# A two-block layer with product-key experts on one core: the last block of weights kept on the chip, three gelu places, and a thinner start of the choice

## What is computed

```python
q = (hb @ w_q).reshape(n, 8, 2, 128)
s = jnp.einsum('nhid,hikd->nhik', q, sub_keys)
s_top, i_top = lax.top_k(s, 16)
cand = s_top[:, :, 0, :, None] + s_top[:, :, 1, None, :]
cand_idx = i_top[:, :, 0, :, None] * 128 + i_top[:, :, 1, None, :]
best, pos = lax.top_k(cand.reshape(n, 8, 256), 16)
idx = jnp.take_along_axis(cand_idx.reshape(n, 8, -1), pos, axis=-1)
w = jax.nn.softmax(best, axis=-1)
u = jnp.take(u_tab, idx, axis=0)
act = jax.nn.gelu(jnp.einsum('nhkd,nd->nhk', u, hb))
out = jnp.einsum('nhk,nhkd->nd', w * act, jnp.take(v_tab, idx, axis=0))
```

## Time and profile before

| | us |
|---|---|
| Median of three runs (3157.71, 3168.16, 3169.7) | 3168.16 |
| The profiled execution: its own time | 3162.28 |
| The profiled execution: its span in the trace | 3160.5 |
| TensorE matmul busy | 3016.7 |
| VectorE busy | 2151.8 |
| ScalarE busy | 1230.4 |
| GpSimd busy | 439.8 |

### The profile page before, as it was taken

The page is one execution under the profiler, slowest core; times in us unless marked ns, Lnnn a source line. Parts: engine busy times, 40 slices in busy tenths (PEclk is TensorE's granted clock), DMA queues, the critical chain, the costliest instruction groups (busy, mean ns, idle before and its releaser), DMA issues. The chain is left out here.

```text
span 3160.5 us, 43420 instructions
## 1 busy us (share of the span) xinstructions
PE 3016.7 (95%) x17739; PEld 2766.1 (88%) x17739; DVE 2151.8 (68%) x3633; ACT 1230.4 (39%) x1936; POOL 439.8 (14%) x296
## 2 busy tenths in 40 slices
PE   7998998999999999999999999899999979999998
PEld 7888887888879888998877879799999979999998
DVE  6446875755643443577663468897987768889897
ACT  2234233222233341555553223366665733333332
POOL 0000000000000000000000000021113335555551
PEclk9888998999999998999999999999999989999999
DMA  6223113223232223212124333558888999999996
GB/s 234 102 101 147 41 44 117 76 91 107 78 130 81 74 107 128 81 68 79 69 100 166 121 120 124 196 203 274 278 268 311 344 359 379 392 392 393 393 392 234
DMA packets 221957, 584.19 MB, mean 185 GB/s; under 512 B 32704, under 2 KB 131520, under 8 KB 186304
## 3 DMA queue, kind: packets, MB, share of 16 engines
q1 hardware_dynamic: 178128, 422.42, 37.3%
q0 software_dynamic: 41472, 151.01, 13.0%
q10 hardware_dynamic: 2160, 7.99, 0.7%
HBM read 510.63 MB, written 70.25 MB: 184 GB/s over the span
## 5 line engine op out<-in xcount | busy, mean ns | idle before, releaser
L591 PE MATMUL bank<-hh,wh 128*128 128x512 f32 (+2 forms) x2512 | 907.8, 361 | 19.7 <-DVE wl L546 9.4
L591 PE MATMUL bank<-hl,wh 128*128 128x512 f32 (+2 forms) x2512 | 878.4, 350 | 0.0
L591 PE MATMUL bank<-hh,wl 128*128 128x512 f32 (+2 forms) x2512 | 877.4, 349 | 0.0
L539 ACT ACTIVATE wh<-ring 128x2048 fp32r<-128x2048 f32 (+2 forms) x249 | 463.6, 1862 | 765.1 <-PE bank L591 756.5
L546 DVE TENSOR_TENSOR wl<-ring,wh 128x2048 fp32r<-128x2048 f32 (+2 forms) x249 | 554.3, 2226 | 299.8 <-ACT wh L539 299.2
L591 PEld LDWEIGHTS bank<-hh,wh 128*128 128x128 f32 x2512 | 481.0, 191 | 70.7 <-issue 18.4
L591 PEld LDWEIGHTS bank<-hl,wh 128*128 128x128 f32 x2512 | 481.2, 192 | 45.7 <-issue 6.0
L591 PEld LDWEIGHTS bank<-hh,wl 128*128 128x128 f32 x2512 | 479.7, 191 | 42.8
L591 PE MATMUL bank<-ph,wh 128*128 128x368 f32 x1024 | 342.8, 335 | 30.8 <-DVE pl L3284 30.8
L591 PE MATMUL bank<-pl,wh 128*128 128x368 f32 x1024 | 340.6, 333 | 0.0
L591 PE MATMUL bank<-ph,wl 128*128 128x368 f32 x1024 | 339.2, 331 | 0.0
(11 more groups left out here) (542 smaller groups left out, 4626.4 us busy)
## 6 DMA issues: line engine op xcount, KB each, us to landing
ring<-in_v SPq DMA_DIRECT2D x68, 1024.0 KB, 15.9
ring<-in_u SPq DMA_DIRECT2D x64, 1024.0 KB, 7.0
ring<-in_ada SPq DMA_DIRECT2D x24, 1024.0 KB, 5.0
gelu_spill<-gst SPq DMA_DIRECT2D x128, 184.0 KB, 4.6
gv<-gelu_spill SPq DMA_DIRECT2D x64, 368.0 KB, 11.6
ring<-in_wup SPq DMA_DIRECT2D x22, 1024.0 KB, 4.8
weight_spill<-stage SPq DMA_DIRECT2D x20, 1024.0 KB, 9.9
wv<-weight_spill SPq DMA_DIRECT2D x64, 320.0 KB, 13.4
```

The costliest lines, as they stand in the source:

```text
L539: a.then_inc(a.e.activation(wh[q % 2][:, 0:n], ring[k % 4][:, 0:n], ACT.Copy), s("whi"))
L591: ins = p.e.matmul(out, l, r, start=start and i == 0, stop=stop and i == len(pairs) - 1, skip_group_check=not check)
```

## The change

`last_weight_spill`, its four writes and its 64 reads go. Block 5 stays where ScalarE put it, in the first 6144 columns of `stage[1]` (`kept`), and `weigh` reads it there. The layout is moved so that nothing writes there before the last `weigh`. The gelu tiles get a third place, in the columns 256 to 623 of `cols`, a constant array whose entries there are no longer needed; `lnfin`, which is needed, is copied away first. The gelu of step t then waits for the spill of step t - 3. In `choose`, `top(0)` and `top(1)` are each put in turn with six empty steps, so that each of their first six steps is followed by an empty one, and CHOOSE goes to 1.33. With it the choice has some 343 steps, and ends two halves behind U instead of with it: VectorE's order now ends `wl` 64, row 111, `wl` 65, `weigh` 0 and 1, `lower` 0. The three fetches stand behind gelu spill 122, the last piece of block 4 behind spill 116, the soft maximum of j = 1 behind gelu 20 instead of 15, the first product of `hot(1)` behind step 27 instead of 21.

```diff
--- before.py
+++ after.py
@@ -318,7 +318,6 @@
     wd_ = nc.dram_tensor("weight_spill", (5, 64, 128, 2, 64), F32).ap()
-    wl_ = nc.dram_tensor("last_weight_spill", (64, 128, 2, TAILS), F32).ap()
@@ -467,6 +466,8 @@
         gst = [sb(f"gst{j}", [128, ND], F32, ar) for j in range(2)]
+        gst.append(cols[:, 256:256 + ND])
+    lnfin = hhu[:, 3, 528:536]
     past = CONST["notfirst"][0]
@@ -478,6 +479,7 @@
     spare = hlu[:, :, 16:16 + GT]
+    kept = flat(stage[1][:, :, :])[:, 0:128 * TAILS].rearrange("p (j t) -> p j t", t=TAILS)
     ijw, nw = spare[:, 0:3, :], spare[:, 7, :]
@@ -490,8 +492,7 @@
         wv = [sb(f"wv{j}", [128, 5, 2, 64], F32, ar) for j in range(3)]
-        wv5 = [sb(f"wv5{j}", [128, 2, TAILS], F32, ar) for j in range(3)]
-        sb("past_choice", [128, 4736 - 12 * ND], F32, ar)
+        sb("past_choice", [128, 4736 - 6 * ND - 1920], F32, ar)
         sb("ub_kept", [128, 2048], F32, ar)
@@ -2887,6 +2888,7 @@
         arrive(v, 8)
+        v.e.tensor_copy(lnfin, cc["lnfin"])
         v.then_inc(v.e.tensor_copy(place, bc(C["iota"][:, 0:16], 128)), s("ve"))
@@ -3005,7 +3007,7 @@
-    WST = 192, 176
+    WST = 192, 128
@@ -3069,7 +3071,7 @@
             if b == 5:
-                place = flat(place)[:, 0:128 * TAILS].rearrange("p (j t) -> p j t", t=TAILS)
+                place = kept
             if q < 31:
@@ -3109,16 +3111,10 @@
     def spill(y, b, z):
-        y.wait_ge(s("stg"), min(16 * b + 16, NQ))
-        landed = s("wfirst") if (b, z) == (5, 0) else s(f"wst{b % 2}")
-        if b == 5:
-            y.e.dma_start(wl_[16 * z:16 * z + 16].rearrange("s i x t -> i s (x t)"),
-                          flat(stage[1][:, :, :])[:, 32 * z * TAILS:32 * (z + 1) * TAILS].rearrange("p (s c) -> p s c", s=16)
-                          ).then_inc(landed.sem, 16)
-            return
+        y.wait_ge(s("stg"), 16 * b + 16)
         y.e.dma_start(wd_[b, 16 * z:16 * z + 16].rearrange("s i x t -> i s (x t)"),
                       stage[b % 2][:, 32 * z:32 * z + 32, :].rearrange("p (s x) t -> p s (x t)", x=2)
-                      ).then_inc(landed.sem, 16)
+                      ).then_inc(s(f"wst{b % 2}").sem, 16)
@@ -3143,14 +3139,18 @@
         yield from turn
-        yield from top(0)
-        yield from top(1)
+        yield from weave((in_turn(top(0), rest(6)), 1))
+        yield from weave((in_turn(top(1), rest(6)), 1))
         yield from weave((hot(1), 1), (top(2), 0.93), (rows(ROWS[0], ROWS[1]), 0.87))
...
+    def rest(n):
+        for _ in range(n):
+            yield
+
     def turn_idle():
@@ -3161,8 +3161,6 @@
         for n in range(n0, n1):
-            if n0 == ROWS[3] and n - n0 == 0:
-                spill(y, 5, 0)
             if n0 == ROWS[3] and n - n0 == 3:
@@ -3206,9 +3204,9 @@
             a.wait_ge(s("u_t"), t + 1)
-            if t >= 2:
-                a.wait_ge(s(f"gst{t % 2}"), 16 * (t // 2))
-            a.then_inc(a.e.activation(gst[t % 2][:, :], bank[t % 4][:, 0:ND], ACT.Gelu_apprx_tanh), s("ge_u"))
+            if t >= 3:
+                a.wait_ge(s(f"gst{t % 3}"), 16 * (t // 3))
+            a.then_inc(a.e.activation(gst[t % 3][:, :], bank[t % 4][:, 0:ND], ACT.Gelu_apprx_tanh), s("ge_u"))
             yield
@@ -3225,10 +3223,10 @@
             y.wait_ge(s("ge_u"), t + 1)
-            y.e.dma_start(gd_[t // 2][:, t % 2, :], gst[t % 2][:, :]).then_inc(s(f"gst{t % 2}").sem, 16)
-            yield
-
-    CHOOSE = 1.28
+            y.e.dma_start(gd_[t // 2][:, t % 2, :], gst[t % 3][:, :]).then_inc(s(f"gst{t % 3}").sem, 16)
+            yield
+
+    CHOOSE = 1.33
@@ -3252,26 +3250,24 @@
             y.wait_ge(s("wst0"), WST[0])
-            y.wait_ge(s("wst1"), 128)
-            y.wait_ge(s("wfirst"), 16)
-            for b in range(2):
-                y.wait_ge(s(f"gst{b}"), 16 * (i + 1))
+            y.wait_ge(s("wst1"), WST[1])
+            for t in (2 * i, 2 * i + 1):
+                y.wait_ge(s(f"gst{t % 3}"), 16 * (t // 3 + 1))
         else:
             y.wait_ge(s("pl"), i - 2)
-            y.wait_ge(s("wst1"), WST[1])
-            for b in range(2):
-                y.wait_ge(s(f"gst{b}"), 16 * (i + 1))
+            for t in (2 * i, 2 * i + 1):
+                y.wait_ge(s(f"gst{t % 3}"), 16 * (t // 3 + 1))
         y.e.dma_start(gv[i % 3][:, :, :], gd_[i]).then_inc(s(f"gv{i % 3}").sem, 16)
...
                       wd_[:, i].rearrange("b i x t -> i b (x t)")).then_inc(s(f"gv{i % 3}").sem, 16)
-        y.e.dma_start(wv5[i % 3][:, :, :], wl_[i]).then_inc(s(f"gv{i % 3}").sem, 16)
...
     def weigh(v, i):
-        v.wait_ge(s(f"gv{i % 3}"), 48 * (i // 3 + 1))
+        v.wait_ge(s(f"gv{i % 3}"), 32 * (i // 3 + 1))
+        v.wait_ge(s("stg"), NQ)
         g4 = gv[i % 3][:, :, 0:320].rearrange("p x (b t) -> p x b t", b=5)
...
         g5 = gv[i % 3][:, :, 320:ND]
-        v.then_inc(v.e.tensor_tensor(g5, g5, wv5[i % 3][:, :, :], M), s("gw"))
+        v.then_inc(v.e.tensor_tensor(g5, g5, kept[:, 2 * i:2 * i + 2, :], M), s("gw"))
@@ -3368,7 +3364,7 @@
                 a.wait_ge(s("gd"), end)
-                a.wait_ge(s("wst1"), WST[1])
+                a.wait_ge(s("wst0"), WST[0])
                 a.then_inc(a.e.activation(to, of, ACT.Gelu_apprx_tanh), s("gg"))
@@ -3376,11 +3372,7 @@
     def start_sy(y):
-        for z in range(1, 4):
-            spill(y, 5, z)
-            yield
-        for _ in range(4):
-            yield
+        yield from start_idle()
@@ -3455,7 +3447,7 @@
         norm_mean(v, 4)
-        norm_ve(v, 4, x3, cc["lnfin"], out=fin)
+        norm_ve(v, 4, x3, lnfin, out=fin)
```

## The result

The changed kernel takes 3141.4 us (median of four runs, 3137.5 to 3143.1) against 3164.4 us before on the same chip: ratio 0.9926, 95% interval 0.9905 to 0.9947, so 0.74% or 23 us faster. The forecast was 3138 with a range of 3116 to 3158. The profiled execution has a span of 3138.0 us (3160.5 before).

| us | before | after | difference | forecast |
|---|---|---|---|---|
| start of U | 1946.5 | 1947.2 | +0.7 | 0 |
| stage U | 636.8 | 624.9 | -11.9 | -11 |
| hole at the seam | 18.8 | 16.3 | -2.5 | -9.5 |
| stage V | 542.1 | 532.9 | -9.2 | -9.5 |
| last V matmul to the end | 16.3 | 16.7 | +0.4 | 0 |

A forecast was written before the change was run, and what follows sets the result against it. DMA was taken to bound V, and TensorE to bound U wherever nothing stops it. Gains of 11 (U), 9.5 (hole) and 9.5 (V) make 30 us: 3132 on the profiled clock, 3138 against the median, range 3116 to 3158.

The forecast's parts named there:

- Stage U, forecast -11: Stage U: thinned first choice steps and the third gelu place make it 11 us shorter, bounds 0 and 19.
- the 3.5 of the sum: Stage U, where `hot(1)` is woven in: VectorE's lateness returns as one longer and one second short stop, 3.5 us lost.
- The hole, forecast 18.8 to 9: TensorE's stop between U and V: earlier fetches cut it from 18.8 to 9 us, 9.5 gained with clock, bounds 0 and 12.
- I add 2 for a gelu spill that lands late among fetches: Between U and V: 2 us allowed for a late gelu spill, on top of a 7 us chain from `wh` to `lower`.
- rival C: Between U and V: gelu spills stick behind the fetches, ScalarE waits as now, no gain there; time 3148, chance 0.10.
- Stage V, forecast -9.5: Stage V: one fetch of 128 x 384 B less per tile saves 9.5 us, bounds 5 and 25.
- 1.7 times: Price of the spill's 384 B packets against price by bytes, from one window; by it V would give 13.7 us.
- B (lateness comes back whole): Stage U: VectorE's lateness returns in full, U gives 0, the rest 19 us; time 3149, chance 0.12.
- D (V gives nothing): Stage V: rows, ring and the 512 B fetch land last instead, gain 20.5 us in all; time 3148, chance 0.10.
- E (the denser weave makes VectorE the bound): Stage U from 2050 to 2350: TensorE loses 23%, 60 us; time 3193, chance 0.05.
- F: Whole kernel: the stops only move and sums cancel, time within 0.5% of before; chance 0.06.
- The forecast's second sum, by DMA alone: From 2554 on, DMA full: less traffic and earlier U, less some 5 us of idle engines, give 28 to 33 us.

The follow-up runs named there:

- the eight kernels: The eight kernels with the changed kernel's V, among them those with moved fetches or without new order or third place; V 527.8 to 533.4 us.

## Why the prediction was right, and where it was not

**Stage U, forecast -11, measured -11.9 in the trace.** The mechanism is right in the profile: in 1980 to 2030 and 2040 to 2050 TensorE stands 0.2 us, its waits for `wl` in 1950 to 2050 are 1.2 us, and the `Ah` stop of 6.8 us is gone. What comes back in 2050 to 2190 is more than the 3.5 of the sum: 5.8 us more idle time than before (140 - 132.47 against 140 - 138.24), 3.09 of it at 2090.84. That the total fits within 1 us is partly luck: seven kernels with this order and three places have U at 626.8 us on average, which is 10 less than before, and they differ by 7.6 among themselves. The sum gave 11.5 less 4.5 to the order and 5 to the third place. Alone they give 4.5 and 3.7, and on the kept block with two places the order gives 2.4 in U and is slower at the median. Single traces with this scatter can't settle whether the parts add in U; that the order leans on the third place is what the waits for `gelu_spill` above and the medians 0.9952 and 0.9926 say together.

**Of these 11.9 us little reaches the end.** The changed kernel is only 2.5 us faster at the median than the kept block alone, whose U is as long as before. From the last U matmul to the end it takes 565.9 us, the other 559.1. So 6.8 of the 11.7 us are given back behind U (hole 16.3 against 14.3, V 532.9 against 529.0, the rest at the end). With the fetches behind spill 124 this part is 558.3 while U stays at 624.8, and the median falls by 8 us. So it is at the seam that the time was lost, as far as this pair tells; how much of it is scatter of V is open, and the kept block alone was not run with the later fetches.

**The hole, forecast 18.8 to 9, measured 16.3: the step that failed.** By the prediction's own sign ("if the first `pl` waits over 15 us") it was wrong here, though the total lies in its range. "I add 2 for a gelu spill that lands late among fetches" was the mis-sized term, some 9 instead of 2; what came is the mechanism of rival C, which had a chance of 0.10. The prediction put the fetches behind spill 122 and let spill 123 follow as if a place in SyncE's order were a place in time. It stands behind 2 MB of fetches on DMA engines which were already full: 21.58 us. And the sum left out the gathers. Fetches that are issued 21 us earlier meet them: q0 moved 5.79 MB while the spill was under way, SyncE's own queue 2.79, where the spill of the earlier trace rows took 8.57 us behind about as much of its own (3.04 MB) with 0.22 MB of gathers. That the place behind the fetches is needed for the delay is shown, since without it no engine waits for a spill; what part the gathers have is read from the queues, and no run moves them. Had that spill been in time, `wh` to `lower` would have run in the 7 us of the sum. Moving only the fetches takes the wait away (12.8), then moving `lower` 0 (9.9) or also splitting the fetches (8.8) brings the rest: the 9 us were there to have, under an order that the change did not make. The term's lower bound, "spill 124 as late as its like now", held the case; the value was taken too near the other end.

**Stage V, forecast -9.5, measured -9.2.** A tile takes 8.29 us (2317 matmuls in 400 us), in the 8.2 to 8.3 that were named. Like U's, this hit is closer than one trace can be read: the mean of the eight kernels is 530.0, which is 12.1 less than before. The extra fetch that puts the bytes back costs 8.5 us, or up to 11.4 by the other readings, so the value taken, between 8.4 by bytes and 13.7 by the spill's dear packets and near the first, holds; the readings lie between the two ends, nearer to the bytes. The 8.4 isn't divided by the share of 1.04 as the 13.7 is; with it the bytes say 8.0. The spill's "1.7 times" was worked out as a remainder of one window and doesn't hold: in the packet records of the trace of before, a 384 B packet of that spill took 23.7 ns on average, a 384 B packet of a fetch in V 24.4 ns, one of 512 B 27.9 ns. Small packets are dear by the byte in both directions, and 8192 of 24.4 ns on 16 engines at 1.04 are an estimated 12.0 us, a little over the readings. The Trainium skill ("DMA: Bandwidth & Descriptors", Specifications) says that below 512 B a transfer pays a read-modify-write. It gives no price; the prediction's estimate with a doubled one was 16 us. All four readings are under that, and no 384 B packet took longer than a 512 B one on average, so a doubled price isn't seen here, and the measurement decides. The same page of the Trainium skill says under "Rules for kernel authors" that below 64 KB one pays mostly overhead. The half-sized fetch leans that way: 7.1 us (6.0 at the medians) for 24.6 KB, where its bytes are 4.2. With traces that scatter by 3 us it doesn't prove it.

**The rivals.** B (lateness comes back whole): not so; over the three windows from 1980 to 2190 TensorE is 83 matmuls ahead (1208 against 1125), 13.8 us at 0.166. D (V gives nothing): not so. E (the denser weave makes VectorE the bound): not so; VectorE is busy 132.6 of 140 us and TensorE does 34 matmuls fewer there (846 against 880), 4% and not 23%. F: not so, but not by much: the gain's interval begins at 0.53%, just above its 0.5%. The forecast's second sum, by DMA alone, "some 5 in which the engines find nothing to do", is the place where the missing time shows as well: a share of 0.86 over the 20 us at the seam.

**The total.** The gain was forecast at 30 us and is 23, of which the hole lacks 7. That the time itself is only 3 us off 3138 is luck: the kernel before came out at 3164.4 with its fourth run, 3.8 under the 3168.2 that the forecast subtracts from.

## What to carry to other kernels

A small store on which an engine waits must not stand behind megabytes of prefetch in one queue, even if it is "only" one place behind; put the prefetch after the last such store, or let only the piece needed first go ahead. Look as well at what other queues move in that stretch: a prefetch brought forward can run into them. A wait removed on one engine (VectorE late) raises the pace to the next limit (two places for a spill): try the second buffer with the new order and not apart from it. And judge a stage's gain by what reaches the end: 11.9 us in U were worth 2.5 at the median here until the order at the seam was changed too.

## What the runs showed of the hardware

- A spill of 184 KB, 4.6 us from issue to landing at the median, took 21.58 us behind 2 MB of fetches while the DMA share was at 1.04 (window 2560 to 2580) and the gathers' queue moved 5.79 MB against 2.79 of SyncE's; the instruction that issued it took 7.58 us instead of 0.32.
- 49 KB more a tile as 64 partitions x 768 B cost 25.1 us over 64 tiles, as 128 x 384 B 8.5 (24.4 and 9.5 at the medians). The share was 1.04 in both, but 381 GB/s were moved instead of 392, and the gathers beside it moved 2.3% less for their share. 64 x 384 B cost 7.1 (6.0 at the medians). The cause isn't settled; no run has the 768 B form on 128 partitions, and no row shows which DMA engines a fetch of 64 partitions uses.
- Packets of 384 B took 24.4 ns on average in V of the kernel before (2650 to 3050), of 512 B 27.9 ns, of 4 KB 166 ns.
- The same code before U ended at 1940.2 to 1952.7 us from kernel to kernel, and the same U order with three places took 624.6 to 632.2: a stage's length in one trace can't tell 3 us here and has to be read beside the medians.
